# Hybrid backbone step: first two units by contraction tiles behind their adaLN pairs, and 1/rms and shift of both MLPs applied behind the first product

## What is computed

```
mods = silu(c) @ w_ada + b_ada                      # shift, scale, gate for mixer and MLP
h = rms_norm(x, w) * (1 + scale) + shift            # adaLN; another scale and shift for the 128 context tokens
x = x + gate1 * (mixer(h @ w_in) @ w_out)
h = rms_norm(x, w2) * (1 + scale2) + shift2
x = x + gate2 * (relu(h @ w_mlp1)**2 @ w_mlp2)      # hidden width 4096
```

## Time and profile before

| what | value |
|---|---|
| median of three runs | 1220.2 us |
| profiled execution | 1220.1 us span, and no other time of it is given |
| PE matmuls | 1092.3 us (90%), 6938 |
| PE weight loads | 988.5 us (81%) |
| DVE, ACT, POOL | 590.0 (48%), 473.9 (39%), 228.2 us (19%) |
| HBM | 160 MB, mean 131 GB/s; 322 in the first slice of 30 us |

### The profile page before, as it was taken

How to read it: one execution, slowest core, us unless ns; L and a number is a source line. 1 busy time by engine, 2 the same in 40 slices (tenths; PEclk the granted TensorE clock), 3 DMA queues, 4 the chain that set the end, 5 groups by cost and what they waited for, 6 DMA issues and landing times.

```text
span 1220.1 us, 17080 instructions
## 1 busy us (share of the span) xinstructions
PE 1092.3 (90%) x6938; PEld 988.5 (81%) x6938; DVE 590.0 (48%) x872; ACT 473.9 (39%) x738; POOL 228.2 (19%) x205
## 2 busy tenths in 40 slices
PE   6599878889776999999999698999786999999998
PEld 2389867655666999999999587787576999999997
DVE  1655757754335544444343725556546443434432
ACT  3355434444432423324242435545632433333241
POOL 0403575401113100001010333113003101000010
PEclk9699989999989999999999899999887999999999
DMA  9756442437542343434434264353212244334321
GB/s 322 251 176 207 139 138 74 138 109 231 162 140 75 101 131 110 138 104 136 138 104 138 73 208 133 119 172 105 91 41 97 75 133 135 117 127 138 104 69 52
DMA packets 157089, 160.23 MB, mean 131 GB/s; under 512 B 3626, under 2 KB 155716, under 8 KB 157028
## 3 DMA queue, kind: packets, MB, share of 16 engines
q1 hardware_dynamic: 155028, 156.50, 39.6%
q0 software_dynamic: 528, 1.70, 0.4%
q10 hardware_dynamic: 1472, 1.18, 0.3%
HBM read 156.09 MB, written 3.28 MB: 131 GB/s over the span
## 4 chain that ended last, share of the span: by engine, by line
PE 76%; DVE 11%; ACT 7%; issue 4%; POOL 2%; DMA 0%; SPq 0%; DVEq 0%; ACTq 0%
PE G L498 54%; PE G L503 7%; PE TB L473 3%; PE OB L519 2%; PE SC L537 2%; ACT wH L921 1%; DVE nbuf L1372 1%; PE OB L822 1%; PE SC L576 1%; DVE E L1474 1%; DVE wL L1337 1%; DVE opL L1380 1%; DVE E L1470 1%; PE OB L624 1%; PE TB L519 1%
## 5 line engine op out<-in xcount | busy, mean ns | idle before, releaser
L498 PE MATMUL G<-opH,wH 128*128 128x384 f32 x768 | 269.1, 350 | 31.2 <-DVE opL L1380 25.7
L498 PE MATMUL G<-opL,wH 128*128 128x384 f32 x768 | 262.5, 342 | 0.0
L498 PE MATMUL G<-opH,wL 128*128 128x384 f32 x768 | 262.2, 341 | 0.0
L921 ACT ACTIVATE wH<-raw 128x2048 fp32r<-128x2048 f32 x93 | 177.6, 1910 | 208.7 <-PE G L498 208.7
L1337 DVE TENSOR_TENSOR wL<-raw,wH 128x2048 fp32r<-128x2048 f32 x93 | 214.8, 2310 | 55.4 <-ACT wH L921 53.7
L498 PEld LDWEIGHTS G<-opH,wH 128*128 128x128 f32 x768 | 148.7, 194 | 40.4 <-issue 25.0
L498 PE MATMUL G<-hidH,wH 128*128 128x384 f32 x512 | 175.6, 343 | 0.0
L498 PE MATMUL G<-hidL,wH 128*128 128x384 f32 x512 | 173.6, 339 | 0.0
L498 PE MATMUL G<-hidH,wL 128*128 128x384 f32 x512 | 173.6, 339 | 0.0
L498 PEld LDWEIGHTS G<-opL,wH 128*128 128x128 f32 x768 | 148.8, 194 | 1.2
L498 PEld LDWEIGHTS G<-opH,wL 128*128 128x128 f32 x768 | 148.5, 193 | 0.0
(11 more groups left out here) (232 smaller groups left out, 1406.2 us busy)
## 6 DMA issues: line engine op xcount, KB each, us to landing
raw<-in_w_mlp SPq DMA_DIRECT2D x64, 1024.0 KB, 5.2
raw<-in_w_ada SPq DMA_DIRECT2D x48, 1024.0 KB, 6.3
raw<-in_w_in_even SPq DMA_DIRECT2D x13, 1024.0 KB, 5.4
raw<-in_w_in_odd SPq DMA_DIRECT2D x12, 1024.0 KB, 5.0
raw<-in_w_out_even SPq DMA_DIRECT2D x4, 1024.0 KB, 5.2
raw<-in_w_out_odd SPq DMA_DIRECT2D x4, 1024.0 KB, 5.0
xin<-in_x_sample SPq DMA_DIRECT2D x1, 1024.0 KB, 6.2
out_y_sample<-yout SPq DMA_DIRECT2D x1, 768.0 KB, 4.0
```

What stands on the lines that cost most here:

```text
L498: mm = pe.matmul(G[:, s, 512 * m:512 * m + NTOK], w[:, s, k, P * m:P * m + P], a[:, k, :], start=first and q == 0, stop=last and q == 2)
L921: act.activation(wH[:, u % 2, :, :], raw[:, pos % RAW, :, :], ACT.Copy).then_inc(w_high, 1)
```

## The change

**Start.** `STREAM` begins with unit 0, then the slices in the order 0, 4, 1, 5, 2, 6, 3, 7 with unit 1 among them and units 2 and 3 behind. The x tiles are turned without slices between them, except slice 0 at the sixth. Then for each pair j: two slices, scale and shift of two tiles, and PE multiplies the two tiles of the pair before with units 0 and 1. Units 2 and 3 now take two slices each (8 to 11). Unit 1 is split by ACT and DVE.

**MLPs.** The operand of the first product is `xT*scale` alone, with no 1/rms and no shift, so it doesn't wait for the norm. The shift goes along as two more columns (one for context, one for latent tokens): the operand is 386 columns wide (`NX`). Behind the product DVE multiplies G with 1/rms, copies the two extra columns to `shifts`, and ACT adds them as bias in the relu, in four instructions instead of one. `opH` tiles are overwritten as soon as the last output unit has read them (`op_read`). The sums of the last two squares stand inside the first MLP unit. Units 18 and 66 are split by ACT and DVE; of `POOL_UNITS` only 50 is left.

```diff
+NX = NTOK + 2
+MLP0_ORDER, MLP1_ORDER = [4, 5, 0, 1, 2, 3, 6, 7], list(range(KT))
+ADA_FIRST = [0, 4, 1, 5, 2, 6, 3, 7]
+def side_adas(u):
+    return [] if u < 2 else [2 * u + 4, 2 * u + 5] if u < 4 else [8 + u]
-STREAM = [("a", a) for a in range(6)] + [("u", 0), ("a", 6), ("a", 7), ("u", 1)]
+STREAM = [("u", 0), ("a", 0), ("a", 4), ("u", 1)] + [("a", _a) for _a in ADA_FIRST[2:]] + [("u", 2), ("u", 3)]
-POOL_UNITS = [1, U_MLP0 + 1, U_ODD + 1, U_MLP1 + 1]
+POOL_UNITS = [U_ODD + 1]
-        opH = sb("opH", [P, KT, NTOK], F32R)
+        opH = sb("opH", [P, KT, NX], F32R)
...
-                if k == 0:
-                    pe.wait_ge(cst_set, 1)
-                ada_mm(k)
                 if k:
                     norm_sum(0, k - 1)
-                ada_turn(k)
+                if k == 5:
+                    pe.wait_ge(cst_set, 1)
+                    ada_mm(0)
...
+            for j in range(1, 4):
+                ada_mm(j)
+                first_tile(0, 2 * j - 2)
+                ada_turn(j)
+                if j < 3:
+                    first_tile(0, 2 * j - 1)
+                ada_mm(4 + j)
+                first_tile(0, 2 * j - 1) if j == 3 else first_tile(1, 2 * j - 2)
+                ada_turn(4 + j)
+                if j == 3:
+                    first_tile(1, 2 * j - 2)
+                first_tile(1, 2 * j - 1)
+            for u in range(2):
+                first_tile(u, 6)
+                first_tile(u, 7)
...
-            last_norm_sums(1)
+                        if first is not None and i == 0 and half == 1:
+                            middle = {1: lambda: norm_sum(first, KT - 2), 2: lambda: norm_sum(first, KT - 1)}
+                        if i < 4:
+                            gemm_half(base + i, half, "fm", (opH, opL), ready, order, g=g, cols=NX, middle=middle)
...
+            def unscaled_high(n, u, order, tiles):
+                layer, freed = n // 2, 7 * (n // 2)
+                if tiles[0] == 0:
+                    act.wait_ge(scale_set, layer + 1)
+                    act.activation(opH[:, :, NTOK:NX], mods[:, layer, KT * SH2:KT * SH2 + KT, :], ACT.Copy)
+                for n_k in tiles:
+                    k = order[n_k]
+                    at = out_order(n).index(k)
+                    if at < KT - 1:
+                        act.wait_ge(op_read, freed + at + 1)
+                    else:
+                        act.wait_ge(gemm_done, u + 1)
+                    if k >= 6:
+                        act.wait_ge(g_free[u % 2], u // 2 + 1)
+                    for c, (a, b) in enumerate(((0, P), (P, NTOK))):
+                        ins = act.activation(opH[:, k, a:b], xT[:, k, a:b], ACT.Copy, scale=scale1[:, n, k, c:c + 1])
+                    ins.then_inc(oph_set, 1)
...
+                if u == 15:
+                    unscaled_high(1, 16, MLP0_ORDER, range(6))
+            unscaled_high(1, 16, MLP0_ORDER, range(6, 8))
+            split(U_MLP0 + 1)
+            squares(1, 16, 6)
             norm_rstd(1)
-            shift(1)
...
-                        act.wait_ge(gemm_done, u + 1 + 8 * g)
+                        act.wait_ge(g_free[u % 2], (u // 2 + 1) + 4 * g)
                         r = relu[:, u % 2, :]
-                        act.activation(r.rearrange("p (m n) -> p m n", m=2),
-                                       G[:, u % 2, :].rearrange("p (m n) -> p m n", m=2)[:, :, 0:NTOK],
-                                       ACT.Relu).then_inc(g_free[u % 2], 1)
+                        for m in range(2):
+                            for c, (a, b) in enumerate(((0, P), (P, NTOK))):
+                                part = relu[:, u % 2, NTOK * m + a:NTOK * m + b]
+                                ins = act.activation(part, part, ACT.Relu, bias=shifts[:, u % 2, m, c:c + 1])
+                        ins.then_inc(relu_set, 1)
...
+            def unscaled_low(n, n_op, order, tiles):
+                layer = n // 2
+                for n_k in tiles:
+                    k = order[n_k]
+                    dve.wait_ge(oph_set, n_op + n_k + 1)
+                    if n_k == 0:
+                        dve.tensor_tensor(opL[:, :, NTOK:NX], mods[:, layer, KT * SH2:KT * SH2 + KT, :],
+                                          opH[:, :, NTOK:NX].bitcast(F32), ALU.subtract)
+                    for c, (a, b) in enumerate(((0, P), (P, NTOK))):
+                        ins = dve.scalar_tensor_tensor(opL[:, k, a:b], xT[:, k, a:b], scale1[:, n, k, c:c + 1],
+                                                       opH[:, k, a:b].bitcast(F32), ALU.mult, ALU.subtract)
+                    ins.then_inc(op_set, 1)
...
+                if u == 15:
+                    unscaled_low(1, 2 * KT, MLP0_ORDER, range(5))
+            dve.wait_ge(g_free[16 % 2], 16 // 2 + 1)
+            unscaled_low(1, 2 * KT, MLP0_ORDER, range(5, 8))
+            split_low(U_MLP0 + 1)
+            dve.wait_ge(rstd_set, 2)
...
+                        dve.wait_ge(gemm_done, u + 1 + 8 * g)
+                        y = G[:, u % 2, :].rearrange("p (m n) -> p m n", m=2)
+                        dve.tensor_scalar(shifts[:, u % 2, :, :], y[:, :, NTOK:NX], 1.0, None, ALU.mult)
+                        dve.tensor_tensor(relu[:, u % 2, :].rearrange("p (m n) -> p m n", m=2), y[:, :, 0:NTOK],
+                                          rstd[:, :].rearrange("p (o n) -> p o n", o=1).broadcast_to([P, 2, NTOK]),
+                                          ALU.mult).then_inc(g_free[u % 2], 1)
```

More of the change, by code:

```diff
@@ L100, in psum_uses @@
     sc.append("norm0")
-    for k in range(KT):
-        tb += [f"x{k}", f"ada{k}"]
-        ob.append(f"ada{k}")
+    tb += [f"x{k}" for k in range(KT)]
+    for a in ADA_FIRST:
+        tb.append(f"ada{a}")
+        ob.append(f"ada{a}")
     def swa(s):
@@ L476, in gemm_half, with gemm_tiles @@
                 gemm_tiles(u, 4 * half, 4 * half + 4, *args, **kw)
-            def gemm_tiles(u, n0, n1, form, moving, ready=None, order=range(KT), g=0, middle={}):
+            def gemm_tiles(u, n0, n1, form, moving, ready=None, order=range(KT), g=0, middle={}, cols=NTOK,
+                           read=None):
                 mH, mL = moving
@@ L497, in gemm_tiles @@
                             for q, (w, a) in enumerate(passes):
-                                mm = pe.matmul(G[:, s, 512 * m:512 * m + NTOK], w[:, s, k, P * m:P * m + P],
-                                               a[:, k, :], start=first and q == 0, stop=last and q == 2)
+                                mm = pe.matmul(G[:, s, 512 * m:512 * m + cols], w[:, s, k, P * m:P * m + P],
+                                               a[:, k, 0:cols], start=first and q == 0, stop=last and q == 2)
                     else:
@@ L507, in gemm_tiles @@
                         mm.then_inc(gemm_done, 1)
+                    elif read is not None:
+                        mm.then_inc(read, 1)
                     if n % 4 in middle:
@@ L707, in out_tiles @@
             def out_tiles(u, n0, n1):
-                gemm_tiles(u, n0, n1, "fm", (opH, opL), op_ready(KT) if u == 13 else None, SWA_FIRST)
+                gemm_tiles(u, n0, n1, "fm", (opH, opL), op_ready(KT) if u == 13 else None, SWA_FIRST,
+                           read=op_read if u == 16 else None)
             def out_half(u, half):
@@ L756, in _, with mlp_group @@
                         norm_sum(1, 2 * (u - 14) + 1)
-            last_norm_sums(1)
-            def mlp_group(base, g, n_op, finish=None):
+            def mlp_group(base, g, n_op, done, order, finish=None, first=None):
                 for i in range(8):
@@ L873, in _ @@
                 for half in range(2):
-                    gemm_half(U_OUT_O + u, half, "fm", (opH, opL))
+                    gemm_half(U_OUT_O + u, half, "fm", (opH, opL), read=op_read if u == 3 else None)
                     if half == 0:
@@ L978, in _ @@
                 square(0, k)
-                if k == 6:
+                if k == 3:
                     split(0)
-                ada_copy(k)
+            ada_copy(0)
             norm_rstd(0)
-            shift(0)
+            ada_copy(4)
+            for j in range(4):
+                if j:
+                    ada_copy(j)
+                    ada_copy(4 + j)
+                shift(0, range(2 * j, 2 * j + 2))
+                if j == 0:
+                    split(1)
             def gates(u):
@@ L1295, in _ @@
                     split(U_OUT_O + u + 2)
-                squares(3, U_OUT_O + u, 2 * u)
+                    squares(3, U_OUT_O + u, 2 * u)
+                if u == 2:
+                    unscaled_high(3, U_OUT_O + 3, MLP1_ORDER, range(6))
+            unscaled_high(3, U_OUT_O + 3, MLP1_ORDER, range(6, 8))
+            split(U_MLP1 + 1)
+            squares(3, U_OUT_O + 3, 6)
             norm_rstd(3)
-            shift(3)
             act.wait_ge(out_dma, 16 * 4)
@@ L1875, in _ @@
             pool.wait_ge(kd_out, 16 * 4)
-            split(U_MLP1 + 1)
             with pool.Fori(0, 4) as g:
```

173 lines of the change are left out of this document (105 added, 68 removed).

## The result

The changed kernel takes 1210.5 us at the median of four runs (1207.0 to 1212.4) against 1220.9 for the kernel before; the ratio is 0.991, 95% interval 0.988 to 0.993. I had forecast 1193.0 and a range from 1185 to 1206, so the time lies outside it: 10 us were gained where I had summed 27. The profiled execution has a span of 1205.2 us against 1220.1: 14.9 less. Spans and times are not the same figure: in every run a time is about 1.8 us above the span of the same execution (1207.0 for 1205.2 here), and the profiled execution of the changed kernel was the fastest of the four.

What follows compares the result with a forecast made beforehand. PE carried 76% of the chain of waits, so time lay only where it stood still or ran at its lower clock. 1220.1 - 12.6 - 13.0 + 1.3 - 2.7 = 1193.1 us, range 1185 to 1206.

Steps and rivals of the forecast that it cites:

- First MLP's seam (12.6): Entry to the first MLP: PE goes straight from unit 16 to unit 17 without waiting for the norm, gain 12.6 us.
- second (13.0): Entry to the second MLP: the same wait for the norm goes, gain 13.0 us.
- wider operand's 1.3: First products of both MLPs: two more columns in each of 1536 matmuls at full clock, cost 1.3 us.
- Rival (c): MLP seams fill only in part, squares or tile 3 late, 3 us each: 1199 us, chance 0.07.
- Hidden units (T+7.7 against T+7.9, cost 0): Unit done at T: low part of unit u+2's weights ready T+7.7, PE wants it T+7.9; room 0.2 us, no cost.
- rival (a): Hidden units' chain a little late, 0.4 us on each of 32 units: up to 1206 us, chance 0.14.
- (d): Hidden units' chain much too late, about 1.1 us: slower than before, 1228 us, chance 0.05.
- a period over 8.5: Hidden units: sign of being wrong if their period exceeds 8.5 us; 8.3 to 8.4 apart was expected.
- The start (gain 2.7): Reordered first units and adaLN slices: unit 3 done at 93.8 us against 96.5, gain 2.7 us.
- Units 2 and 3 with four slices: 16.6 + 5.9 - 0.4: Start, after the pause before unit 2: time for two units with four slices, 16.6 + 5.9 - 0.4 us.
- my sign of 97: Start: sign of being wrong if unit 3 is done later than 97 us.
- (b): Start: the pairs of k-tiles run at the low clock, 9.7 us later, 1203 us in all, chance 0.10.

Runs made afterwards that it cites:

- cols_384: Changed kernel with first slice reduced early and unit 2's weights split before unit 0's gates, but streaming 384 columns in the first product, not 386: 1187.4 us, single time.
- double_mult: Changed kernel with first slice reduced early and unit 2's weights split before unit 0's gates, plus each hidden unit's 1/rms multiplication done twice: 1197.3 us, ratio 0.981.
- turn_early: Changed kernel, but in units 2 and 3 DVE reduces the first of two adaLN slices ahead of its scans: 1194.6 us, ratio 0.978 to the kernel before.
- mlp_only: Kernel before with both MLPs and their seams as changed, but the old start, transfer order and POOL split of unit 1: 1197.5 us, ratio 0.983.

## Why the prediction failed, step by step

- **First MLP's seam (12.6), second (13.0): right.** Steps of 9.76 and 9.89 at full clock, and PE waits for nothing in between. With the wider operand's 1.3 I summed 24.3, and 23.6 came. Rival (c) is out. One reading in it was wrong and no term of the sum: the four DVE instructions of 5.66 us (389.81 to 395.47) stood beside POOL's rounding only for their first half microsecond, and for the rest mostly beside its subtraction, timeline of the kernel before:

```profile
390.43 4.50 POOL L1726 TENSOR_TENSOR wL<-raw,wH 128x2048 fp32r<-128x2048 f32 x1
```

- **Wider operand (1.3): wrong in size, nearly right in sum.** Between the two kernels the first product moved by 4.2 ns a matmul for 0.83, 6.5 us over 1536, and the hidden operand gave back 5.1 (3.3 ns over 1536), so the net is 1.4. Only 1.8 ns of the 4.2 go with the two columns (cols_384). That the sum came out is luck of the layout, not my reason.
- **Hidden units (T+7.7 against T+7.9, cost 0): right**, chain at T+7.6, multiplication 0.95. The bound of T+7.9 was too early: low parts at T+8.43 cost 0.2 a unit (double_mult). The 0.2 of room which gave rival (a) its 0.14 and (d) its 0.05 was too small. My sign of being wrong, a period over 8.5, did come (8.53 in the first MLP), yet not by the chain: 48 matmuls at 177.6 ns are 8.52.
- **The start (gain 2.7): the step that failed.** It failed in "Units 2 and 3 with four slices: 16.6 + 5.9 - 0.4". What stood ahead of it was right within 3 us, on the good side: unit 0 done at 59.8 for 62.4, the pause 4.76 for 4.7, unit 2 begun at 66.6 for 69.2, cold loss 2.5 for 2.3. In that sum I took the price of a slice from units that carry one. A unit with two needs `TB` twice, and the first transposes stay there till DVE reads them, behind `forget`. Two waits of 3.90 and two spells at half clock, 1.9 and 1.5: 11.2 us. Unit 3 was done at 98.4 for 93.8, past my sign of 97, and unit 4, for which I had no term, lost the second wait. Without the waits (turn_early), two units with four slices would have stood as summed: units 2 and 3 end 11.26 apart in it, which is 8.32 + 2 x 1.47. (Added up again, 69.2 + 2.3 + 16.6 + 5.9 - 0.4 is 93.6 and not 93.8; the 0.2 changes nothing.)
- **The sum.** By the profile 12.1 us are missing: 10.3 at the start (2.7 expected, 7.6 lost), 0.7 in the MLPs and 1.1 in the odd layer. The medians miss more, 1210.5 for a forecast of 1193.0: 17.5. Of the 5.4 us beyond the 12.1, 1.8 are that I added up spans and forecast a time, and 3.4 that the profiled execution is the fastest of four (1207.0). Rivals (a), (c) and (d) stayed away; of (b) one spell came, the clock at 0.50 from 31.7 to 38.5, with 7 matmuls near 320 ns and a slice's sixteen in 1.94 us for 1.07, some 1.9 us by these figures; the one that came, a wait that takes the place of those removed, I had put only ahead of unit 2.
- **The range and chances.** I gave the start's lower bound as a loss of 7 by the low clock; the loss of 7.6 came, from another cause. The profiled span (1205.2) is just under the bound of 1206, but the time of that same execution, 1207.0, is not, and the median even less. Runs of the changed kernel spread over 5 us, with the mean clock from 0.957 to 0.966: I let the span of one execution of before stand for the median of the times, and did not ask how firm that is for a kernel with other pauses.

## What to carry to other kernels

When side work is doubled in one stage, don't multiply its price: walk through every buffer that it passes and ask who empties it between the first and the second use, and what that engine does first. A single-buffered bank whose reader stands behind the main chain's work is a wait in waiting, and its repair is one moved step (13 us at that point here, for a restructured start that lost 7 us without it). Then time the repaired part against a kernel without the part: here the repaired start is 3.5 to 5.6 us ahead at unit 4, and by spans and times turn_early can't be told from mlp_only. When several changes are tried at once, time them apart: here one part was worth -25.7 us and the other +6.7, by spans. And count a pause of TensorE twice, once for itself and once for what the clock takes behind it.
